# One step of a hybrid decoder layer: weights and token tiles in another order at the start, and rotary keys gathered sixteen to a row

## The reference

```
h @ w_in, of which first:   c_q (384), c_kv (256), k_r (32)       # 672 columns, D_MODEL = 1024 rows
ckv = concatenate([cache_ckv[layer, pt].reshape(past, KV_LORA), cn])      # pt: 32 pages of 128 positions
kr  = concatenate([cache_kr[layer, pt].reshape(past, ROPE_DIM), kn])      # 4096 positions x 32
scores = einsum("bqhc,btc->bhqt", q_lat, ckv) + einsum("bqhr,btr->bhqt", q_rope, kr)
p = softmax(where(mask, scores * MLA_SCALE, NEG_INF));  o = einsum("bhqt,btc->bqhc", p, ckv)
```

## Time and profile before

| | us |
|---|---|
| median of 3 runs | 1380.05 (1379.93 to 1382.51) |
| the profiled execution | 1370.07 |
| its span, first to last instruction | 1368.2 |
| PE busy in it | 1328.9 (97%) |
| DVE, ACT, POOL busy in it | 846.6, 518.2, 214.9 |

### The profile page before, as it was taken

How to read it: one execution, slowest core, us unless ns; L and a number is a source line. 1 busy time by engine, 2 the same in 40 slices (tenths; PEclk the granted TensorE clock), 3 DMA queues, 4 the chain that set the end, 5 groups by cost and what they waited for, 6 DMA issues and landing times.

```text
span 1368.2 us, 27314 instructions
## 1 busy us (share of the span) xinstructions
PE 1328.9 (97%) x11072; PEld 1181.3 (86%) x11072; DVE 846.6 (62%) x1669; ACT 518.2 (38%) x1105; POOL 214.9 (16%) x161
## 2 busy tenths in 40 slices
PE   7999999999998999989999999999999999999997
PEld 7999977766756676659999999999999999999785
DVE  4376458887597777465866767644444454668655
ACT  4221467676372433353333334333333341213100
POOL 3110028777422433010000000000000000000000
PEclk9999999999999999999999999999999999999999
DMA  6643120000392677791221131234233346542722
GB/s 225 214 135 119 29 92 2 1 1 0 95 356 68 244 267 287 264 332 47 63 80 48 47 95 47 63 96 125 90 104 109 97 164 225 196 156 84 256 95 75
DMA packets 102272, 174.19 MB, mean 127 GB/s; under 512 B 15650, under 2 KB 74722, under 8 KB 96772
## 3 DMA queue, kind: packets, MB, share of 16 engines
q1 hardware_dynamic: 96004, 134.70, 29.9%
q0 software_dynamic: 6144, 37.75, 7.5%
HBM read 138.37 MB, written 34.06 MB: 126 GB/s over the span
## 4 chain that ended last, share of the span: by engine, by line
PE 55%; DVE 0%; issue 0%; ACT 0%; DVEq 0%
PE ps L2533 37%; PE ps L2564 10%; PE ps L2598 7%; PE ps L2584 1%; DVE p_h L2906 0%; DVE p_h L2909 0%; DVE p_stats L2893 0%; DVE p_h L2889 0%; PE ps L2574 0%; DVE p_mv L2900 0%; ACT p_rt L2681 0%; DVE p_rs L2904 0%; DVE p_stats L2898 0%; DVE p_stats L2897 0%; DVE p_ve L2902 0%
## 5 line engine op out<-in xcount | busy, mean ns | idle before, releaser
L2533 PE MATMUL ps<-p_x,p_w 128*128 128x272 f32 x4032 | 508.3, 289 | 1.1 <-PEq L2064 0.8
L2533 PEld LDWEIGHTS ps<-p_x,p_w 128*128 128x128 f32 x4032 | 507.9, 189 | 1.5 <-issue 1.5
L2564 PE MATMUL ps<-p_uh,p_w 128*128 128x352 f32 (+1 forms) x576 | 141.9, 327 | 0.0
L2783 DVE TENSOR_TENSOR p_w<-p_sum,p_w 128x512 fp32r<-128x512 f32 x94 | 64.9, 691 | 118.9 <-ACT p_w L1991 118.8
L1055 POOL TENSOR_SCALAR p_pr<-p_pr,p_rec 128x896 f32<-128x896 f32 (+3 forms) x64 | 112.3, 1765 | 127.9 <-DVE p_rec L1017 127.6
L1991 ACT ACTIVATE p_w<-p_wr 128x512 fp32r<-128x512 f32 x96 | 60.1, 626 | 131.4 <-PE ps L2564 76.0
L2564 PEld LDWEIGHTS ps<-p_uh,p_w 128*128 128x128 f32 x576 | 101.8, 188 | 0.0
L2564 PE MATMUL ps<-p_ul,p_w 128*128 128x352 f32 (+1 forms) x288 | 94.4, 328 | 0.0
L2783 DVE TENSOR_TENSOR p_w<-p_wr,p_w 128x512 fp32r<-128x512 f32 x95 | 65.5, 689 | 38.1 <-ACT p_w L1991 37.5
L1107 DVE STREAM_TRANSPOSE p_kT<-p_rawc 128x1024 f32<-128x1024 f32 x64 | 76.1, 1223 | 14.1 <-DMA p_rawc<-cache_ckv,p_rows 13.8
L1991 ACT ACTIVATE p_w<-p_sum 128x512 fp32r<-128x512 f32 x96 | 59.8, 623 | 17.8 <-PE ps L2533 11.9
(11 more groups left out here) (340 smaller groups left out, 2400.2 us busy)
## 6 DMA issues: line engine op xcount, KB each, us to landing
p_wr<-w_in SPq DMA_DIRECT2D x48, 512.0 KB, 3.6
g_kept<-p_slots SPq DMA_DIRECT2D x48, 272.0 KB, 2.5
p_ring<-g_kept SPq DMA_DIRECT2D x16, 544.0 KB, 4.8
p_x<-x_kept SPq DMA_DIRECT2D x6, 1088.0 KB, 8.7
t_kept<-p_t_raw SPq DMA_DIRECT2D x16, 272.0 KB, 2.4
p_x<-t_kept SPq DMA_DIRECT2D x4, 1088.0 KB, 8.4
p_gy<-g_kept SPq DMA_DIRECT2D x8, 544.0 KB, 5.8
p_xs<-x_prompt SPq DMA_DIRECT2D x8, 512.0 KB, 4.2
```

The costliest lines, as they stand in the source:

```text
L2533: last = pe.matmul(ps[:, lo + z, 0:PW], w[:, q % NW, part, t, :], v[:, t, z * PW:(z + 1) * PW], start=(i in STARTS and t == 0 and n == 0), ...
L2564: last = pe.matmul(ps[:, BANK_OF[g % 8], 0:tn], w[:, q % NW, part, t, :], v[:, t0:t0 + tn], start=(t == 0 and z == 0), stop=(t == KH - 1 a ...
L2783: dve.tensor_tensor(w[:, q % NW, 1], w_source(e, q), f32(w[:, q % NW, 0]), ALU.subtract).then_inc(w_lo, 1)
```

## The change

At the start: tile 0 is loaded in two halves of its columns, with a semaphore for the first (`x_first`), and its first four transposes need only that one. SP loads weight 0, then tile 1, then weights 1 to 7. PE goes weight by weight: tile 0 and tile 1 by weight 0, both by weight 1, and so on; turn(2) follows weight 3 and turn(3) weight 5. ACT and DVE split tile 0, weight 0, tile 1, weights 1 to 7, tiles 2 and 3. DVE first clears 512 columns of a weight buffer that is not in use yet, and PE multiplies these zeros into bank 7, twice ahead of tile 0 and twice after turning tile 1; the results are overwritten.

In the decode stage rotary keys are gathered 16 positions (ROTK) to a row, 2 KB, in 16 gathers into two slots of the double size. A row of the page table entry now belongs to 8 partitions, not 16, so the table comes in by 16 loads of 8 x 16 numbers instead of 8 of 16 x 32, and the numbers for the latents' rows (`rows`, two for each of rotary's) are made from `rot_rows` on DVE.

```diff
@@ project_latents
+        blank = f32(wlq[:, KT - 1, 0:BANK])
...
-                sp.dma_start(xs[0:rows(i), i % 2, :], src).then_inc(x_in[i % 2], 16)
+                if i == 0:
+                    sp.dma_start(xs[:, 0, 0:D // 2], src[:, 0:D // 2]).then_inc(x_first, 16)
+                    sp.dma_start(xs[:, 0, D // 2:D], src[:, D // 2:D]).then_inc(x_in[0], 16)
+                else:
+                    sp.dma_start(xs[0:rows(i), i % 2, :], src).then_inc(x_in[i % 2], 16)
             x_dma(0)
-            for u in range(4):
-                w_dma(u)
+            w_dma(0)
             x_dma(1)
-            for u in range(4, KT):
+            for u in range(1, KT):
                 w_dma(u)
...
+            def idle_products(count):
+                for _ in range(count):
+                    pe.matmul(ps[:, 7, :], blank[:, 0:P], blank[:, :], start=True, stop=True)
+
+            pe.wait_ge(blanked, 1)
+            idle_products(2)
+            pe.wait_ge(consts, 16)
             turn(0)
             turn(1)
-            for i in range(NT):
-                latents(i)
+            idle_products(2)
+            for t in range(KT):
+                latents(0, [t])
+                latents(1, [t])
+                if t == 3 or t == 5:
+                    turn(2 + (t - 3) // 2)
+            for i in range(2, NT):
+                latents(i, range(KT))
                 if i + 2 < NT:
                     turn(i + 2)
...
+            dve.memset(blank[:, :], 0.0).then_inc(blanked, 1)
@@ the decode stage's gathers
-ROWK, NH, NAT, RAWR = 8, NG // 2, 10, 4
-RPP = PAGE // ROWK
+ROWK, NH, NAT = 8, NG // 2, 10
+ROTK, NR, RAWR = 2 * ROWK, NH // 2, 2
+RPP = PAGE // ROTK
...
-def gather_rotary(nc, a, e, h):
-    rows_in = a["cache_kr"].rearrange("o n (p a) c -> (o n p) (a c)", a=ROWK)
+def gather_rotary(nc, a, e, r):
+    if r >= RAWR:
+        nc.gpsimd.wait_ge(e["keys_done"], 2 * (r - RAWR) + 2)
+    rows_in = a["cache_kr"].rearrange("o n (p a) c -> (o n p) (a c)", a=ROTK)
...
-            for j in range(ROWK):
-                src = a["page_table"].rearrange("b (q j) -> j (b q)", j=ROWK)[j:j + 1, :].broadcast_to([RPP, NH])
+            for j in range(ROTK):
+                src = a["page_table"].rearrange("b (q j) -> j (b q)", j=ROTK)[j:j + 1, :].broadcast_to([RPP, NR])
...
+            dve.wait_ge(rot_rows_done, 1)
+            for s in range(2):
+                last = dve.tensor_scalar(e["rows"][:, :, s], e["rot_rows"][:, :], 2.0, float(s), ALU.mult, ALU.add)
...
             for h in range(NAT):
                 gather_pages(nc, a, e, h)
+            gather_rotary(nc, a, e, RAWR)
...
-                if RAWR <= h < NH:
-                    pool.wait_ge(keys_done, h - RAWR + 1)
-                    gather_rotary(nc, a, e, h)
-
-            fetch(RAWR)
             for n in range(0, NG, S):
                 pool.wait_ge(scored, n // S + 1)
                 fetch(n // 2 + 5)
+                if n // S + RAWR + 1 < NR:
+                    gather_rotary(nc, a, e, n // S + RAWR + 1)
                 fetch(n // 2 + 6)
```

More of the change, by code:

```diff
@@ L254, in turn, with latents @@
                 last.then_inc(turned, 1)
[L256 removed]
+            def latents(i, chunks):
                 r, b = rows(i), 4 + 2 * (i % 2)
                 tok = slice(i * P, i * P + r)
[L259 to L263 removed]
+                if 0 in chunks:
+                    pe.wait_ge(xh_done, i + 1)
+                    pe.wait_ge(xl_done, i + 1)
+                    if i >= 2:
+                        pe.wait_ge(kept, i - 1)
+                for t in chunks:
                     if i == 0:
@@ L320, in _ @@
             x_hi(0)
-            for u in range(4):
+            w_hi(0)
+            x_hi(1)
+            for u in range(1, KT):
                 w_hi(u)
-            x_hi(1)
-            for u in range(4, KT):
-                w_hi(u)
+            x_hi(2)
+            x_hi(3)
             act.wait_ge(zeroed, 2)
             for i in range(NT):
-                if i + 2 < NT:
+                if 2 <= i < NT - 2:
                     x_hi(i + 2)
@@ L390, in _ @@
             x_lo(0)
-            for t in range(4):
+            w_lo(0)
+            x_lo(1)
+            for t in range(1, KT):
                 w_lo(t)
-            x_lo(1)
-            for t in range(4, KT):
-                w_lo(t)
+            x_lo(2)
+            x_lo(3)
             for i in range(NT):
@@ L1416, in _ @@
             pool.wait_ge(rows_done, 1)
-            for h in range(RAWR):
-                gather_rotary(nc, a, e, h)
+            for x in range(RAWR):
+                gather_rotary(nc, a, e, x)
             pool.wait_ge(kv_done, 4)
```

58 lines of the change are left out of this document (30 added, 28 removed).

## The result

The changed kernel takes 1373.28 us (median of 4 runs, 1372.48 to 1377.12), the kernel before on the same chip 1381.13 (4 runs). Timed once more on another occasion it was 1374.79 against 1382.66, ratio 0.9945 (0.9927 to 0.9963).

The account below looks back on a forecast made before the run. TensorE, busy 97%, was taken as the bound, so only its earlier start counts: beginning 3.0 us, rotary keys and page table 0. From 1370.07 to 1367.1 profiled, plus the 10 us distance: 1377.0, range 1375.5 to 1380.5.

Parts of the forecast that it names:

- What bounds the kernel: Whole kernel: TensorE busy 97%, no idle time mid-decode, so cheaper transfers or vector operations there gain nothing; earlier TensorE work does.
- Rotary keys, worth 0: Decode stage: 32 rotary gathers become 16, 16 us less POOL work on a mostly idle engine; worth 0, far end 0.5 us.
- Rival E: Decode stage start: fewer packets let pages land earlier, gaining up to 1.90 us more, total 1375.1; chance 0.08.
- The distance of 10 us between profiled execution and median: Whole kernel: the unprofiled median 1380.05 lies 10 us above the profiled 1370.07; left as it is.
- The beginning, 3.0 us: Start of kernel: first product of tile 2 at 27.6 instead of 30.60, 3.0 us earlier, arriving whole at the end.
- rival B: Beginning: clock fallen or never risen when tile 1 comes, gain only 1.1 us, total 1378.9; chance 0.22.
- Landing: Beginning: tile 1, with one weight ahead instead of four, lands at 8.2 us, bounds 7.6 to 8.9.
- The way from the first product to tile 2: Beginning: 16 weight steps, 14.94 us, and turns of tiles 2 and 3, 1.58; tile 2 starts at 27.6 when banks are free.
- The row of 1.90: Decode stage: the clock outlived a 1.90 us TensorE wait, taken as evidence for the higher clock from tile 1 on.
- Clock: Beginning: blank products keep the higher clock from tile 1 on; at the far end 1.1 of the 3.0 us remain.
- Page table, banks, splits: Sixteen table loads instead of eight cost zero; tile 2's banks free at 27.56 us; ACT and DVE splits keep up at the beginning.
- Rival D: Decode stage: POOL's rotary waits on two slots delay page gathers, half a microsecond per 13 iterations, total 1383.6; chance 0.06.

Follow-up runs that it names:

- before again: The kernel before, unchanged, run and profiled once more: span of the profiled execution 1380.4 us, median 1381.17 us, ratio 0.9987 to the kernel before.
- beginning alone: The kernel before with only the changed beginning (loads, weight by weight, blank products), rotary gathers as before: 1382.56 us, ratio 1.0000.
- Rotary alone: The kernel before with only the rotary gathers of 16 positions, beginning as before: 1371.48 us, ratio 0.9928; timed again 1370.00 us, ratio 0.9915.
- e13: Kernel before with half the rotary gathers, issued behind the second page gather; from the fifth on, eight GpSimd memsets replace each: 1373.26 us, ratio 0.9931.
- e14: Kernel before with half the rotary gathers, issued behind the second page gather; from the fifth on, plain GpSimd transfers of 128 consecutive rows: 1368.05 us, ratio 0.9894.

## Why the prediction was wrong

- **What bounds the kernel.** The prediction took no idle time of TensorE in the middle of the decode stage for proof that nothing which gets cheaper there buys anything. This step failed. TensorE really did not stand still in the execution that it read, but in before again it did for 8.1 us and in the beginning alone for 7.7, and the view of busy time, which counts a stalled product as busy, shows hardly a difference. That the executions without a trace stalled too is argued from their times, all of them at least 8.7 us longer. What stands ahead of the prediction, that no other engine holds TensorE up where it shows no idle time, fails by the same rows.
- **Rotary keys, worth 0.** The failed term. It weighed POOL's 16 us only as work on an idle engine and looked for who waits for its results. The cost was in another engine's stream beside the issue. Rotary alone measured 11.2 us (and 12.9 the second time), far outside the term's 0.5. Rival E had the sign, by a mechanism (pages landing earlier) that no run shows: DVE's waits for pages are 14.2 us in the changed kernel, 13.8 in the earlier trace rows and 10.8 in before again. Its 1375.1 also lay below the stated range, which stopped at 1375.5.
- **The distance of 10 us between profiled execution and median, which the prediction left as it was.** This was mostly the stall: 11.8 of the 12.2 us between the spans of that execution and before again lie in the decode stage. The profiled execution lacked what the change removes (169.5 us there, 171.7 in the changed kernel, 181.3 in before again), and the text carried the difference along as a constant.
- **The beginning, 3.0 us.** Mis-sized by the clock, as rival B had it: 1.0 measured at tile 2 against the earlier trace rows. Landing (8.43 for 8.2) and mechanism were right. The way from the first product to tile 2 was put at 16.8 us and took 17.3, so that with the clock kept (beginning alone, tile 2 at 28.20) the gain against the earlier trace rows is 2.4. And the base was late: against before again, whose tile 1 was turned at 10.33 and not at 11.52, it is zero in the changed kernel (134.11 and 134.07 at the next stage), and 1.4 with the clock kept (132.70). Nothing of it is clear of the noise at the end. The row of 1.90 did not decide the clock: behind the same blank products and turn, a wait of 1.82 us kept it and waits of 2.05 and 2.53 lost it. What parts them no run shows.
- **Clock.** The changed kernel was granted 0.50 from 9 to 12 us in both of its traces, the beginning alone 1.00 (first product at 10.88). The Trainium skill (TensorE: Matmul & The Clock Gate, "HAM oscillation"), which was weighed in the forecast, describes a kernel that falls back to the low clock in its waits for transfers. The waits there are longer than these; the two traces look like it, the third does not.
- **Page table, banks, splits: right.** SP took 10.62 us where it had taken 10.88; tile 2 waits 0.19 us for the copies; TensorE has no other wait between 13 and 30 us.
- **Rival D** did not occur in the changed kernel: its rotary waits, 5.83 and 6.63 us, lie at the stage's start, with no page gather late behind them.

## What to carry to other kernels

Before a forecast rests on one profiled execution, hold its time against the median of the other runs. A distance of 0.7%, as here, can be a stage that behaves otherwise, and it may be the one that the change touches. In full stretches count instructions, not busy time. In this kernel gathers by a list of rows cost nothing beside longer products (in before again 32 of 128x256 took 3.67 us with two issues beside them at 470.61, and 3.67 with none at 590.89) and up to 2.3 us beside 64 short ones. And one with a wait of its own, put ahead of others on the same engine, held them all up.

## What the runs showed of the hardware

- While GpSimd issues a gather by a list of rows (0.91 to 1.03 us, for 16 or 128 rows, 128 bytes or 8 KB each), a stream of 64 short TensorE products (29 to 31 ns apart) runs dry, in 17 of the 20 traces: 0.4 to 0.7 us of issue beside them cost 0.1 to 0.6 us, two issues 0.8 to 2.3. Memsets and a plain transfer issued by GpSimd in the same place (e13, e14, one trace each) cost nothing.
- One traced execution of the kernel before had the same issues at nearly the same places and no stall, and it was 8.7 us faster than any of over a hundred others. Why is open.
- The granted clock can stand near 0.50 for several microseconds in one execution of a kernel and not in another, near 200 us in 14 of 20 traces and between 604 and 634 in 15. In the twelve runs of before again a mean lower by 0.001 went with about 1 us (1378.9 at 0.998, 1384.3 at 0.992).
